# Recurrence levels of 32 tokens and fewer on four 32-column groups of the array, with four masked copies a level

## The chip, the cores and the metric
The program runs on one core of a Trainium2 chip. The metric is the time of one execution on the device in microseconds (us), smaller being better. Before the change three runs gave a median of 1046.14 us (1046.14 to 1046.6). The execution that was profiled took 1045.28 us.

## The reference, cut to what matters
The kernel computes two layers of a hybrid encoder over 512 tokens of width 1024. The part in question is branch C, a gated linear recurrence with 4 heads, key and value width 128, in chunks of 64 tokens:

```python
bcum = jnp.cumsum(gc, axis=2)                     # cumulated log decay in a chunk
diff = bcum[:, :, :, None, :] - bcum[:, :, None, :, :]
decay = jnp.where(causal, jnp.exp(jnp.where(causal, diff, 0.0)), 0.0)
attn = jnp.sum(qc[:, :, :, None, :] * kc[:, :, None, :, :] * decay, axis=-1)
o = einsum('bhts,bhse->bhte', attn, vc) + einsum('bhtd,bhde->bhte', qc * exp(bcum), state)
```

So `attn[t, s]` is a sum over 128 channels of query times key times a decay that depends on both tokens and on the channel.

## The kernel before, in words
Everything is written out by hand for each engine, with semaphores between them. Per layer TensorE runs a list of projection jobs (`JOBS`), most of them 24 matmuls of 128 stationary columns with 512 moving ones (48 with 256 moving ones for `ci` and `bv`, 12 for `mix`), each fp32 product being made of three fp32r matmuls (L480, L481, L482). Results alternate among three PSUM banks `pj`. Between job n and job n+1 TensorE takes the small stages whose turn it is (`hooks[n]`), so these stand in line with the jobs. VectorE (DVE), ScalarE (ACT) and GpSimd (POOL) have lists of phases with the same numbers. `claim` (L474) waits, at the start of a job, for its weights and its bank.

The intra-chunk matrix `attn` is built by levels. For two heads at a time (p = 0, 1) the kernel works on blocks of 128 tokens, two heads by four blocks, so `2 * TB` = 8 blocks, numbered `hb`. Level `lev` has s = 64 >> lev: within each aligned block of 2s tokens it gives the pairs (key in the lower half, query in the upper half). The decay is split at the boundary between the halves: `diffs` (DVE, L1365, L1366), `decay_exp` (ACT, L901) and `operands` (DVE, L1378, L1381) write `XL[lev % 2]`, tile `level_ops`, in which every token's column holds its scaled key or its scaled query. `level` (L587 to L609) on TensorE multiplies them. Level 0 has a form of its own (L599). Levels 1 to 6 (L607) take, for each block `hb` and each half of it, the 64 columns of that half as the stationary operand and the 32 query columns among them as the moving one; the product lands in 64 PSUM partitions and 32 columns of bank `M[3 + lev % 2]`, tile `mx`. Only the entries in which key and query share a block of 2s tokens are wanted.

`take_level` (L1397 to L1420) on DVE copies them into `AT` (tile `attnT`), one `copy_predicated` for each half (L1418): 64 partitions by 8 blocks by 32 columns, with the mask `mask(lev)` of `constants()`, which holds a 1 where the entry is wanted. The other entries stay as they are.

The stages go by job number. With d = 12 for p = 0 and d = 25 for p = 1, the levels follow job d + 1 (diagonal and level 0), d + 3 (levels 1 and 2), d + 5 (levels 3 and 4) and d + 7 (levels 5 and 6), as `PAIRS` says. Their copies stand in DVE's phase with the next number, and behind those of levels 1 to 4, in the same phase, the operands of the next pair, which PE wants two jobs after this one. After the last copies DVE scales keys and queries (`decayed`, L1438, L1440), and TensorE transposes the keys two jobs after the last levels (L616). Before each level `level` waits for `ops_ready` and, for levels 1 to 6, for `at_evac` (L602): that the level two before has been copied out of the bank.

With two layers, two values of p and six levels, L607 is passed 24 times, 16 matmuls each. The operands are plain fp32, and the trace shows such a matmul as two weight loads and two matmuls: 24 x 16 x 2 = 768 of each.

Of the kernel before, what the change touches and what calls it, by code (L numbers as in the profile page):

```python
# [24 lines left out]
P = 128  # L25
KT = D // P
TB = T // P
# [32 lines left out]
GATE_JOBS = [n for n in SG_JOBS if KIND[n] != "bu"]  # L60
BRANCH = {"ag": 0, "bg": 1, "cg": 2}
LEVELS = 7
DIAG = (12, 25)
PAIRS = ((0,), (1, 2), (3, 4), (5, 6))

# [12 lines left out]
def constants():  # L78


    c = np.zeros((P, P + 8 * LEVELS + 8), np.float32)
    masks = c[:, P:P + 8 * LEVELS].view(np.uint8)
    c[:, 0:P] = np.eye(P)
    for lev in range(1, LEVELS):
        s = 64 >> lev
        for i in range(P):
            if i % (2 * s) < s:
                b = i % 64 // (2 * s)
                masks[i, 32 * lev + b * s:32 * lev + (b + 1) * s] = 1
    o = P + 8 * LEVELS  # L90
    freq = np.float32(ROPE_THETA) ** (-np.arange(0, HD, 2, dtype=np.float32) / np.float32(HD))
    c[:, o] = np.tile(freq, P // (HD // 2))
    c[:, o + 1] = np.where(np.arange(P) % HD < HD // 2, -2.0, 2.0)
    return c


def build(nc, x, positions, w_in, b_merge, w_branch, w_out, norm_g, final_g, attn_sinks, sp_w, sp_b,
# [9 lines left out]
    with ctx:  # L107
# [8 lines left out]
        def at(name, shape, offset, dt=f32):  # L116
            return nc.alloc_sbuf_tensor_at(name, shape, dt, offset=offset)
# [44 lines left out]
        AT = at("attnT", [P, 2, T], r_at)  # L162
# [44 lines left out]
        ID = CST[:, 0:P]  # L207
        FREQ, SIGN2 = (CST[:, P + 8 * LEVELS + c:P + 8 * LEVELS + c + 1] for c in (0, 1))

        def mask(lev):  # L210
            return CST[:, P + 8 * lev:P + 8 * (lev + 1)].bitcast(mybir.dt.uint8)
# [11 lines left out]
        def sem(name):  # L223
# [7 lines left out]
            exp_done=4, probs_ready=4, pT_done=4, pT_evac=4, pv_done=4, oa_evac=4, first_zero=1, sig_ready=2,  # L231
            logf_ready=2, c_keys=2, diff_done=2 * LEVELS + 2, decay_ready=2 * LEVELS + 2, ops_ready=2 * LEVELS,
            lev_done=2 * LEVELS + 2, at_evac=2 * LEVELS + 2, khat_ready=2, khT_done=2, khT_evac=2, upd_done=2,
# [150 lines left out]
        def x_bank(k):  # L384

            return (M[2:] + PJ)[k % 6]
# [51 lines left out]
        def _(pe):  # L438

            pe.wait_ge(cst_in, 16)  # L440
            for k in range(KT):
# [5 lines left out]
                for tb in range(TB):  # L447
                    last = pe.transpose(x_bank(k)[:, tb * P:(tb + 1) * P], XTOK[:, tb, k * P:(k + 1) * P], ID)
# [6 lines left out]
            def program(layer):  # L455
# [133 lines left out]
                def level(p, lev):  # L589
                    s = 64 >> lev  # L590
                    pe.wait_ge(ops_ready, upto(ops_ready, LEVELS * p + lev + 1))
                    ops = XL[lev % 2]
                    bank = M[3 + lev % 2]
                    if lev == 0:

                        for hb in range(2 * TB):
                            low, up = (ops[:, hb * P + u * 64:hb * P + u * 64 + 64] for u in range(2))
                            rows = slice(hb % 2 * 64, hb % 2 * 64 + 64)
                            last = pe.matmul(bank[rows, hb // 2 * 64:hb // 2 * 64 + 64], low, up, start=True, stop=True)  # L599
                        last.then_inc(lev_done, 1)  # L600
                        return
                    pe.wait_ge(at_evac, upto(at_evac, (LEVELS + 1) * p + lev))  # L602
                    for hb in range(2 * TB):
                        for half in range(2):
                            blk = ops[:, hb * P + half * 64:hb * P + half * 64 + 64]
                            upper = blk.rearrange("p (b u s) -> p b u s", u=2, s=s)[:, :, 1, :]
                            last = pe.matmul(bank[half * 64:half * 64 + 64, hb * 32:(hb + 1) * 32], blk, upper,  # L607
                                             start=True, stop=True)
                    last.then_inc(lev_done, 1)  # L609

# [79 lines left out]
                for j in range(4):  # L690
                    hooks[ATTN + 3 * j].append((scores, j))
                for p, d in enumerate(DIAG):
                    hooks[d + 1].append((diagonal, p))
                    for i, levels in enumerate(PAIRS):
                        for lev in levels:
                            hooks[d + 1 + 2 * i].append((level, p, lev))
                    for step, f in enumerate((transpose_khat, state_updates, recurrent_out, head_norm)):
                        hooks[d + 2 + LEVELS + step].append((f, p))
# [31 lines left out]
                for n in range(NJ):  # L730
# [7 lines left out]
                    if n == 0:  # L738
# [4 lines left out]
                        for tb in range(TB):  # L743
                            last = pe.matmul(M[3][:, tb:tb + 1], SS[:, tb * P:(tb + 1) * P], ONE[:, 0:1],
                                             start=True, stop=True)
# [9 lines left out]
        def _(act):  # L755
# [50 lines left out]
            def program(layer):  # L806
# [196 lines left out]
                for j in range(4):  # L1003
                    phase[ATTN + 3 + 3 * j].append((probsT_out, j))
                    phase[ATTN + 1 + 3 * j].append((softmax_exp, j))
                for p, d in enumerate(DIAG):
                    phase[FIRST[("cf", p)] + 2].append((forget, p))
# [122 lines left out]
        def _(dve):  # L1130
# [35 lines left out]
            for c, cn, r0 in ((0, 8, 0), (8, 24, 16), (32, 4, 64)):  # L1166
                last = dve.tensor_copy(VL[:, :, c:c + cn],
                                       M[0][:, r0:r0 + 2 * cn].rearrange("p (l c) -> p l c", l=2))
# [60 lines left out]
            def program(layer):  # L1229
# [170 lines left out]
                def take_level(p, lev):  # L1400
                    s = 64 >> lev
                    dve.wait_ge(lev_done, upto(lev_done, (LEVELS + 1) * p + lev + 2))
                    dve.wait_ge(at_evac, upto(at_evac, (LEVELS + 1) * p + lev + 1))
                    src = M[3 + lev % 2]
                    if lev == 0:
                        at5 = AT[:, :, :].rearrange("p h (c v t) -> p (h c) v t", v=2, t=P)
                        for v in range(2):
                            last = dve.tensor_copy(at5[0:64, :, v, 64:128],
                                                   src[v * 64:v * 64 + 64, 0:4 * 64].rearrange("p (c t) -> p c t", t=64))
                        last.then_inc(at_evac, 1)  # L1410
                        return
                    nb = 32 // s
                    at6 = AT[:, :, :].rearrange("p h (c v b u s) -> p (h c) v b u s", v=2, u=2, s=s, b=nb)
                    for half in range(2):
                        rows = slice(half * 64, half * 64 + 64)
                        msk = mask(lev)[rows, :].rearrange("p (b s) -> p b s", s=s).unsqueeze(1)\
                                                .to_broadcast([64, 2 * TB, nb, s])
                        last = dve.copy_predicated(at6[rows, :, half, :, 1, :], msk,  # L1418
                                                   src[rows, 0:2 * TB * 32].rearrange("p (c b s) -> p c b s", b=nb, s=s))
                    last.then_inc(at_evac, 1)  # L1420

                def block_diffs(p):
# [135 lines left out]
                for j in range(4):  # L1558
                    phase[ATTN + 1 + 3 * j].append((neg_max, j))
                for p, d in enumerate(DIAG):  # L1560
                    phase[FIRST[("cf", p)] + 2].append((clamp, p))
                    phase[FIRST[("cf", p)] + 3].append((keys_and_sums, p))
                    phase[d - 1].append((diffs, p, 0))
                    phase[d].append((diffs, p, 1))
                    phase[d].append((operands, p, 0))
                    phase[d + 1].append((operands, p, 1))
                    phase[d + 1].append((diffs, p, 2))
                    phase[d + 2].append((take_diagonal, p))
                    phase[d + 2].append((take_level, p, 0))
                    phase[d + 2].append((operands, p, 2))  # L1570
                    for i in (1, 2):
                        for lev in PAIRS[i + 1]:
                            phase[d + 1 + 2 * i].append((diffs, p, lev))
                        for lev in PAIRS[i]:
                            phase[d + 2 + 2 * i].append((take_level, p, lev))
                        for lev in PAIRS[i + 1]:
                            phase[d + 2 + 2 * i].append((operands, p, lev))
                    phase[d + LEVELS].append((block_diffs, p))
                    for lev in PAIRS[3]:
                        phase[d + LEVELS + 1].append((take_level, p, lev))  # L1580
                    phase[d + LEVELS + 1].append((decayed, p))
                    phase[d + LEVELS + 4].append((states, p))
                    phase[d + LEVELS + 6].append((head_scaled, p))
# [14 lines left out]
                for n in range(NJ + 4):  # L1598
# [9 lines left out]
                    v = layer * NU + JOBS[n][0] + 1 if n < NJ and JOBS[n][1] == 0 else 0  # L1608
# [34 lines left out]
```

## Time and profile before

| | |
|---|---|
| median of three runs | 1046.14 us |
| the profiled execution | 1045.28 us |
| its span, first to last instruction | 1043.4 us |
| TensorE (PE) busy | 1018.4 us, 98% |
| DVE busy | 650.5 us, 62% |
| ACT busy | 521.0 us, 50% |
| mean granted TensorE clock | 0.996 of full |

The span lies inside the execution; 1.9 us of the profiled execution are around it. In the profile PE is TensorE's matmuls, PEld its weight loads, PEldq its sequencer, which passes the instructions on to the array and takes the waits. A row of groups reads: line, engine, operation, tile written <- tiles read, shape, count | busy time, mean of one | idle time before. A matmul's printed duration runs to a modelled end and overlaps its neighbours; what it costs the array is seen from start to start, or in the chain.

### The profile page before, as it was taken

The page shows a single profiled execution, that of the slowest core. Times are in us where ns is not written, and L with a number is a line of the kernel's source. Part 1 is how long each engine was busy: PE and PEld are TensorE (multiplying, and loading weights), DVE is VectorE, ACT ScalarE, POOL GpSimd, SP SyncE. Part 2 cuts the span into 40 slices and gives each one's busy share as a digit, 9 for nine tenths or more (in the row PEclk, how much of TensorE's full clock was granted, in tenths as well). Part 3 has the DMA queues.
Part 4 walks back from the last instruction along what each step waited for, and adds up shares of the span by engine and source line. Part 5 has one row for each costly group of instructions (what it writes and reads, how often), then busy time and mean ns, then how long its engine had stood idle before and what let it go on. Part 6 is the DMA issues. An engine that isn't in the chain of part 4 may idle for free.

```text
span 1043.4 us, 15327 instructions
## 1 busy us (share of the span) xinstructions
PE 1018.4 (98%) x6389; PEld 857.8 (82%) x6389; DVE 650.5 (62%) x832; ACT 521.0 (50%) x809; POOL 302.8 (29%) x156
## 2 busy tenths in 40 slices
PE   5899999999999999999999999999999999999997
PEld 4689899888888888888887889988888888888876
DVE  6876894799635444355548579578984353544552
ACT  5667665676453323232448666577556333332333
POOL 3321111532422313143212110163243232323420
PEclk9899999999999999999999999999999999999999
DMA  6242222222223232333234222122231232323502
GB/s 196 71 129 74 81 83 82 60 62 82 82 61 120 82 101 82 100 101 122 84 114 136 81 83 59 64 82 81 82 101 57 85 102 81 101 81 101 191 12 80
DMA packets 95412, 94.71 MB, mean 91 GB/s; under 512 B 2272, under 2 KB 93616, under 8 KB 95344
## 3 DMA queue, kind: packets, MB, share of 16 engines
q1 hardware_dynamic: 95136, 93.44, 28.9%
q8 instruction: 50, 0.82, 0.3%
q0 software_dynamic: 80, 0.26, 0.2%
q14 instruction: 18, 0.15, 0.1%
q10 hardware_dynamic: 128, 0.04, 0.0%
HBM read 91.64 MB, written 2.10 MB: 90 GB/s over the span
## 4 chain that ended last, share of the span: by engine, by line
PE 95%; DVE 2%; issue 1%; ACT 1%; DMA 1%; POOL 0%; DVEq 0%; POOLq 0%; ACTq 0%
PE pj L480 28%; PE pj L482 27%; PE pj L481 27%; PE mx L607 2%; PE mx L480 1%; PE mx L482 1%; PE mx L481 1%; DVE sum_sq L1196 1%; PE mx L570 1%; PE mx L667 1%; PE mx L547 1%; PE mx L635 1%; PE mx L555 1%; PE mx L645 1%; DMA pos_int<-in_positions 1%
## 5 line engine op out<-in xcount | busy, mean ns | idle before, releaser
L1066 POOL TENSOR_TENSOR w_lo<-w_raw,w_hi 128x512 fp32r<-128x512 f32 (+1 forms) x92 | 198.5, 2158 | 564.5 <-ACT w_hi L783 564.3
L480 PE MATMUL pj<-h_hi,w_hi 128*128 128x512 f32 x832 | 330.7, 397 | 1.5 <-issue 1.5
L482 PE MATMUL pj<-h_hi,w_lo 128*128 128x512 f32 x832 | 325.1, 391 | 0.0
L481 PE MATMUL pj<-h_lo,w_hi 128*128 128x512 f32 x832 | 325.0, 391 | 0.0
L783 ACT ACTIVATE w_hi<-w_raw 128x1024 fp32r<-128x1024 f32 (+1 forms) x184 | 160.6, 922 | 164.3 <-PE pj L482 162.4
L1187 DVE TENSOR_TENSOR w_lo<-w_raw,w_hi 128x512 fp32r<-128x512 f32 (+1 forms) x92 | 159.8, 1737 | 64.9 <-ACT w_hi L783 64.7
L480 PEld LDWEIGHTS pj<-h_hi,w_hi 128*128 128x128 f32 x832 | 156.9, 189 | 36.5 <-issue 4.6
L482 PEld LDWEIGHTS pj<-h_hi,w_lo 128*128 128x128 f32 x832 | 156.7, 188 | 33.3
L481 PEld LDWEIGHTS pj<-h_lo,w_hi 128*128 128x128 f32 x832 | 157.0, 189 | 32.3 <-issue 1.0
L1253 DVE TENSOR_TENSOR merge_gate<-pj,rstd 128x512 f32<-128x512 f32 x48 | 33.2, 691 | 162.9 <-PE pj L482 162.9
L863 ACT ACTIVATE merge_gate<-merge_gate,small 128x512 f32<-128x512 f32 x48 | 34.3, 715 | 89.3 <-DVE merge_gate L1253 89.3
L480 PE MATMUL pj<-branch_hi,w_hi 128*128 128x512 f32 x192 | 75.1, 391 | 0.0
L482 PE MATMUL pj<-branch_hi,w_lo 128*128 128x512 f32 x192 | 74.8, 389 | 0.0
L481 PE MATMUL pj<-branch_lo,w_hi 128*128 128x512 f32 x192 | 74.7, 389 | 0.0
L480 PE MATMUL pj<-w_hi,h_hi 128*128 128x256 f32 x256 | 73.9, 289 | 0.0
L481 PE MATMUL pj<-w_lo,h_hi 128*128 128x256 f32 x256 | 72.4, 283 | 0.0
L482 PE MATMUL pj<-w_hi,h_lo 128*128 128x256 f32 x256 | 72.4, 283 | 0.0
L1066 POOL TENSOR_TENSOR branch_lo<-full,branch_hi 128x512 fp32r<-128x512 f32 x24 | 36.0, 1500 | 94.0 <-ACT branch_hi L950 80.5
L480 PEld LDWEIGHTS pj<-w_hi,h_hi 128*128 128x128 f32 x256 | 49.0, 191 | 0.7
L481 PEld LDWEIGHTS pj<-w_lo,h_hi 128*128 128x128 f32 x256 | 49.0, 192 | 0.0
L482 PEld LDWEIGHTS pj<-w_hi,h_lo 128*128 128x128 f32 x256 | 49.0, 191 | 0.0
L901 ACT ACTIVATE decay<-decay 128x1024 f32<-128x1024 f32 x28 | 29.6, 1067 | 32.9 <-DVE decay L1366 32.2
(240 smaller groups left out, 1526.2 us busy)
## 6 DMA issues: line engine op xcount, KB each, us to landing
w_raw<-in_w_in SPq DMA_DIRECT2D x60, 1024.0 KB, 5.5
w_raw<-in_w_branch SPq DMA_DIRECT2D x24, 512.0 KB, 3.4
w_raw<-in_w_out SPq DMA_DIRECT2D x6, 1024.0 KB, 5.1
x_tokens<-in_x SPq DMA_DIRECT2D x4, 512.0 KB, 9.0
w_raw<-in_w_in SPq DMA_DIRECT2D x4, 512.0 KB, 4.0
w_raw_last<-in_w_out SPq DMA_DIRECT2D x2, 1024.0 KB, 7.3
sp_w_rows<-in_sp_w SPq DMA_DIRECT2D x2, 512.0 KB, 4.7
out<-out_low SPq DMA_DIRECT2D x4, 256.0 KB, 2.0
```

Source lines behind the costliest of these rows:

```text
L480: pe.matmul(bank, wh, ah, start=first, stop=False)
L481: pe.matmul(bank, wh, al, start=False, stop=False)
L482: return pe.matmul(bank, wl, ah, start=False, stop=final)
L547: last = pe.matmul(M[half][rows, cols], QP[d, j, queries], keys[d, held], start=True, stop=True)
L555: last = pe.transpose(M[half][:, tb * P:(tb + 1) * P], PR[:, half, tb, :], ID)
L607: last = pe.matmul(bank[half * 64:half * 64 + 64, hb * 32:(hb + 1) * 32], blk, upper, start=True, stop=True)
L783: act.activation(hi_part(v, half), raw_part(v, half), ACT.Copy).then_inc(w_hi, 1)
L863: act.activation(GM[:, i % 2, t, :], GM[:, i % 2, t, :], ACT.Sigmoid, bias=bm[:, c:c + 1])\
L901: act.activation(E[lev % 2][:, :], E[lev % 2][:, :], ACT.Exp).then_inc(decay_ready, 1)
L1066: return pool.tensor_tensor(out=dst, in0=full, in1=hi.bitcast(f32), op=ALU.subtract)
L1187: dve.tensor_tensor(out=lo_part(v, 1), in0=raw_part(v, 1), in1=hi_part(v, 1).bitcast(f32), op=ALU.subtract).then_inc(w_lo_vec, 1)
L1253: dve.tensor_tensor(out=GM[:, i % 2, t, :], in0=src, in1=RS[:, :], op=ALU.mult)\
```

## The change
Levels 2 to 6 (s of 16 and fewer, so blocks of 32 tokens and fewer) go in quarters of a block of 128 tokens: 32 stationary columns, 16 moving ones, the output in 32 PSUM partitions, so that the four quarters lie on four column groups of the array. DVE takes each of these levels with four `copy_predicated` of 32 partitions. Level 1 stays as it was, level 0 and the diagonal too. In the mask only the number of the column at which a block's entries stand changes.

```diff
+TILE = (P, 64, 32, 32, 32, 32, 32)
@@ constants
-                b = i % 64 // (2 * s)
+                b = i % TILE[lev] // (2 * s)
@@ level, TensorE
+                    w = TILE[lev]
                     for hb in range(2 * TB):
-                        for half in range(2):
-                            blk = ops[:, hb * P + half * 64:hb * P + half * 64 + 64]
+                        for q0 in range(0, P, w):
+                            blk = ops[:, hb * P + q0:hb * P + q0 + w]
                             upper = blk.rearrange("p (b u s) -> p b u s", u=2, s=s)[:, :, 1, :]
-                            last = pe.matmul(bank[half * 64:half * 64 + 64, hb * 32:(hb + 1) * 32], blk, upper,
+                            last = pe.matmul(bank[q0:q0 + w, hb * w // 2:(hb + 1) * w // 2], blk, upper,
                                              start=True, stop=True)
@@ take_level, VectorE
-                    nb = 32 // s
-                    at6 = AT[:, :, :].rearrange("p h (c v b u s) -> p (h c) v b u s", v=2, u=2, s=s, b=nb)
-                    for half in range(2):
-                        rows = slice(half * 64, half * 64 + 64)
-                        msk = mask(lev)[rows, :].rearrange("p (b s) -> p b s", s=s).unsqueeze(1)\
-                                                .to_broadcast([64, 2 * TB, nb, s])
-                        last = dve.copy_predicated(at6[rows, :, half, :, 1, :], msk,
-                                                   src[rows, 0:2 * TB * 32].rearrange("p (c b s) -> p c b s", b=nb, s=s))
+                    w = TILE[lev]
+                    nb = w // 2 // s
+                    at6 = AT[:, :, :].rearrange("p h (c v b u s) -> p (h c) v b u s", v=P // w, u=2, s=s, b=nb)
+                    for v in range(P // w):
+                        rows = slice(v * w, v * w + w)
+                        msk = mask(lev)[rows, 0:w // 2].rearrange("p (b s) -> p b s", s=s).unsqueeze(1)\
+                                                       .to_broadcast([w, 2 * TB, nb, s])
+                        last = dve.copy_predicated(at6[rows, :, v, :, 1, :], msk,
+                                                   src[rows, 0:TB * w].rearrange("p (c b s) -> p c b s", b=nb, s=s))
```

## Rows read from the trace of the kernel before

**Rows 1.** The page: busy times, and the chain that ended last by engine
```profile
PE 1018.4 (98%) x6389; PEld 857.8 (82%) x6389; DVE 650.5 (62%) x832; ACT 521.0 (50%) x809; POOL 302.8 (29%) x156
...
PE 95%; DVE 2%; issue 1%; ACT 1%; DMA 1%; POOL 0%; DVEq 0%; POOLq 0%; ACTq 0%
```

**Rows 2.** Chain of waits around levels 1 and 2: start us, us, what
```profile
129.73 0.88 PE mx L555 x8
130.61 1.99 PE mx L607 x64
132.59 0.31 PE pj L480
```

**Rows 3.** Groups by line and shape, PE and PEld, line L607
```profile
L607 PE MATMUL mx<-level_ops 128*64 128x32 f32 x768 | 24.6, 223 | 0.0
...
L607 PEld LDWEIGHTS mx<-level_ops 128*64 128x64 f32 x768 | 23.4, 138 | 2.7 <-issue 2.4
```

**Rows 4.** Timeline of PE from 130.53, windows ending at 130.58, 130.66, 130.72
```profile
130.54 0.25 PE L607 MATMUL mx<-level_ops 128*64 128x32 f32 x2
...
130.54 0.31 PE L607 MATMUL mx<-level_ops 128*64 128x32 f32 x4
...
130.54 0.37 PE L607 MATMUL mx<-level_ops 128*64 128x32 f32 x6
```

**Rows 5.** Timeline of PE at 76 us: L547, tiles of 64 rows by 64 columns
```profile
76.25 0.32 PE L547 MATMUL mx<-k_rot,q_rot 64*64 64x128 f32 x1
76.26 0.32 PE L547 MATMUL mx<-k_groups_swapped,q_rot 64*64 64x128 f32 x1
76.27 0.27 PE L547 MATMUL mx<-k_rot,q_rot 64*64 64x64 f32 x1
76.27 0.27 PE L547 MATMUL mx<-k_groups_swapped,q_rot 64*64 64x64 f32 x1
...
77.07 0.27 PE L547 MATMUL mx<-k_groups_swapped,q_rot 64*64 64x128 f32 x2
```

**Rows 6.** Stretches, L547 alone, then L607 alone: us, busy (count started), clock
```profile
76.25:76.92 0.67, 0.67 (x34) 0.67 (x38) 1.00 0.00 0
...
115.97:117.00 1.03, 1.02 (x44) 0.91 (x44) 1.00 0.65 119
...
130.53:130.92 0.39, 0.38 (x14) 0.39 (x14) 1.00 0.32 18
```

**Rows 7.** The sequencer's waits (L302 after L547, L602, L577, L302 after L599): duration, start
```profile
L302 PEldq EVENT_SEMAPHORE  x1: 51/51/51, 76.9 to 76.9; - x1
...
L602 PEldq EVENT_SEMAPHORE  x1: 51/51/51, 130.9 to 130.9; - x1
...
L577 PEldq EVENT_SEMAPHORE  x1: 51/51/51, 116.6 to 116.6; - x1
...
L302 PEldq EVENT_SEMAPHORE  x1: 51/51/51, 117.9 to 117.9; - x1
```

**Rows 8.** Chain where levels 5 and 6 follow L570, another 64-column stage
```profile
161.13 1.08 PE mx L570 x32
162.21 1.84 PE mx L607 x64
```

**Rows 9.** DVE by line: the masked copies in two stretches, and plain operations
```profile
L1418 DVE COPY_PREDICATED attnT<-consts,mx x4: 427/438/452, 136.8 to 138.2; 64x256 f32<-64x256 uint8 x4
...
L1418 DVE COPY_PREDICATED attnT<-consts,mx x4: 737/742/747, 163.2 to 165.5; 64x256 f32<-64x256 uint8 x4
...
L1408 DVE COPY attnT<-mx x8: 415/420/425, 121.3 to 723.0; 64x256 f32<-64x256 f32 x8
...
L1394 DVE TENSOR_TENSOR attnT<-mx,consts x8: 683/689/694, 119.8 to 721.8; 64x512 f32<-64x512 f32 x8
```

**Rows 10.** Stretch of p = 1's levels: us, busy us of PE, PEld, DVE, ACT, POOL
```profile
225.00:255.00 30.00, 30.00 (x276) 24.52 (x277) 29.27 (x37) 19.15 (x19) 9.15 (x4) 1.00 0.23 71
```

**Rows 11.** Timeline of DVE: operands of levels 3 and 4, then 5 and 6
```profile
236.29 2.88 DVE L1381 TENSOR_TENSOR level_ops<-query_c,decay 128x512 f32<-128x512 f32 x1
...
250.49 2.89 DVE L1381 TENSOR_TENSOR level_ops<-query_c,decay 128x512 f32<-128x512 f32 x1
```

**Rows 12.** Chain: where PE takes those two pairs of levels
```profile
241.15 1.99 PE mx L607 x64
...
254.24 1.99 PE mx L607 x64
```

**Rows 13.** Timeline after the last levels of p = 1: DVE, then PE
```profile
258.81 3.07 DVE L1418 COPY_PREDICATED attnT<-consts,mx 64x256 f32<-64x256 uint8 x4
261.91 1.20 DVE L1438 TENSOR_TENSOR key_c<-key_c,decay 128x384 f32<-128x384 f32 x2
263.03 1.21 DVE L1440 TENSOR_TENSOR query_c<-query_c,decay 128x1024 f32<-128x1024 f32 x1
...
267.18 0.82 PE L616 MATMUL mx<-consts,key_c 128*128 128x128 f32 x6
```

## Prediction

> **What bounds the kernel now.** The page comes first: PE is busy for 98% of the span and holds 95% of the chain that ended last, DVE is busy for 62% [rows 1]. So a microsecond that TensorE spends in a small stage between two projection jobs is a microsecond of the end, unless an idle time of PE later on takes it up, and all its idle time together is 25 us (1043.4 of the span less 1018.4). Next the chain around a pair of levels: 64 records of L607 in a row, 1.99 us, and then the next job at once [rows 2]. There are 12 such pairs. The groups by line give L607 24.6 us in all for 768 matmul records [rows 3], 32 ns each, and this is all that the change can touch on PE. Its halves already run side by side: by 130.58 two records have started, by 130.66 four, by 130.72 six [rows 4], so two records (one for each column group) start every 0.06 us. The clock is at its full level (2.4 GHz, granted 1.00) in such stretches [rows 6].
>
> **Part 1, TensorE.** Removed: in 20 of the 24 levels, 16 matmuls, which are 32 records of weight load and 32 of matmul. Added: 32 matmuls, 64 and 64 records, each with half the columns on both sides. The question is what a record costs when it is that small and four of them may run at once. No row shows 32 columns, so I bound it.
>
> From below: a round of two column groups takes 0.058 us with 64 columns (64 records, 32 rounds, in about 1.86 us). If a round of four groups with 32 columns took half of that, 0.029 us, a level would be 16 rounds, 0.47 us in place of 0.93. From above: if a record cost what it costs now, 0.029 us, a level would take 64 x 0.029 = 1.86 us.
>
> What decides is how fast the sequencer hands instructions to the array: a level becomes 128 instructions in place of 64. Now 64 instructions in 0.93 us are 14.6 ns each. For 0.47 us they would have to come every 3.6 ns. L547 is the nearest case, since four tiles run at once there: four records of it start within 0.02 us [rows 5]. It has 44 matmuls and 44 loads [rows 6], 88 instructions. At 76.92 us 34 and 38 of them had started [rows 6], 16 were left, and at 76.9 the sequencer was taking the wait that stands behind all 88 [rows 7]. In the levels, where the array is the slower one, the sequencer runs further ahead: at 130.9 it takes the wait of the second level [rows 7] with 28 of the first level's 64 started [rows 6], so with 36 in the queue. I read 36 as the queue's fill when it is full. At 76.25 then at most 36 of the 88 were in it, and the other 52 or more went in during 0.67 us: 12.9 ns each, or 12.2 if it held 33. The second reading: between the waits L577 at 116.6 and L302 at 117.9 [rows 7] lie L585 and L599, 96 instructions, and one wait of 51 ns: (1.3 - 0.05) / 96 = 13.0 ns, with the starts printed to a tenth. There the array could have been what limited, so this is a ceiling of the price. I take 12.5 ns an instruction. That is below the 14.6 ns at which the levels drain now, which is why the limit hasn't shown; it is three times what four groups would ask for.
>
> A pair of levels with 32 columns (3 and 4, 5 and 6; 8 pairs): 256 instructions, 34 of them queued when the first starts, and one wait of 51 ns between the levels. 222 x 12.5 + 51 = 2.83 us from first to last start, against 1.84 (1.99 less the 0.15 of the change of tile shape at its edge; the pair that follows another 64-column stage shows 1.84 [rows 8]). That is +0.99 us, times 8 = +7.9 us.
>
> The pair of levels 1 and 2 (4 of them): level 1 drains as now, 0.93 us, and leaves the queue full. Then the tile shape changes from 64 to 32 columns, for which I take the 0.15 us by which the two pairs of [rows 2, 8] differ. Level 2 then needs (128 - 34) x 12.5 = 1.18 us in place of 0.93. Together +0.4 us each, +1.7 us. And the two pairs that follow L570 [rows 8] now have a change of shape in front of them as well: +0.3 us. Sum on PE: **+9.9 us**.
>
> At 9.4 ns an instruction, the mean over L547 with the head start in it (88 from 76.25 to its last starts near 77.08 [rows 5], 0.83 us), the same sums give +0.3 us for each of the 8 pairs and +0.1 for each of the 4, so +3. At today's 14.6 ns they give +1.45 and +0.6, with the shapes +14.3. Those are the ends for this case.
>
> The Trainium skill, "TensorE: Matmul & The Clock Gate", has in its part on the warmup a floor under small matmuls: start to start never drops below about 25 ns however few columns there are. L547 disagrees as far as it goes (44 records in 0.83 us are 19 ns each, with a full queue at its start); with that floor at every record a level would take 64 x 25 = 1.6 us, and 20 levels would add some 13 us by estimate, which lies inside the ends above.
>
> **Part 2, VectorE.** Removed: 40 copies of 64 x 256. Added: 80 of 32 x 128 elements each. Two plain operations give the parts of a duration: 420 ns for 256 elements, 689 for 512 [rows 9], so 151 ns fixed and 1.05 ns an element. The masked copies take 438 ns at the larger s and 742 at s of 2 and 1 [rows 9]; with half the elements about 295 and 447. Four in place of two: 1.18 for 0.88 us, 1.79 for 1.48, so +0.3 us a level, +6 us of DVE in all, on an engine with 390 us to spare. From the other side, at least nothing, and at most +0.9 us a level if 32 partitions cost as much as 64 x 256. I cost it at nothing for the end, but the cover is thin at p = 1, where DVE is busy for nearly all of the stretch [rows 10]. Two places count. The operands of levels 5 and 6 are ready at 253.38 [rows 11] and PE takes them at about 254.2 [rows 12], 0.8 us later. By then DVE has three more such levels behind it, +0.9 us, while PE has become later by its own pairs 1, 2 and 3, 4, +0.4 and +1.0. So PE comes 1.3 us after them instead of 0.8, and no wait appears; at the dear end (+2.7 us) PE would wait 0.5 us, once a layer. For levels 3 and 4 the gap is 2.0 us (239.17 to 241.15 [rows 11, 12]) against +0.3. Behind the last copies stand L1438 and L1440, which end at 264.24, and the transposes of these keys start at 267.18 [rows 13]: 2.9 us for 0.6 of copies (1.8 at the dear end).
>
> **Part 3, the rest.** The mask has the same size and is built on the host. No DMA, no wait and no order of stages changes.
>
> Sum: the profiled execution's own 1045.28 us + 9.9 = 1055.2. The median of the runs is 0.9 above that execution, so I forecast 1046.14 + 9.9 = **1056.0 us**.
>
> **The rivals.**
> Gain: four groups side by side at the price of their columns. For it: the array overlaps tiles, two in L607 and four in L547 [rows 4, 5], and bursts of records a few ns apart are seen. Against it: the lag of the sequencer behind 88 instructions [rows 6, 7]. It decides if an instruction can be handed over in under 8 ns; there 222 x 8 + 51 ns is today's 1.84. At its best: 16 levels x -0.47 = -7.5, four times -0.47 + 0.15 = -1.3, and +0.3 for shapes: -8.5. But then PE reaches levels 5 and 6 of p = 1 1.2 us earlier (0.3 and 0.9) while DVE is 0.9 later, against 0.8 of cover: PE waits 1.3 us there, in both layers, and gives back 2.6. That leaves -5.9: 1040.2 us. The Trainium skill's same page, in the part on packing small matmuls, speaks for this side: column groups with 32 columns ran at 2.38 times the rate with three tiles. Its case had 512 moving columns, where this one has 16.
> No change: only two of four groups overlap, with half the columns. 32 rounds x 0.029 = 0.93 us, as now, and four changes of shape: +0.9 us, 1047.0. It needs both a quick sequencer and an array that doesn't do four; nothing speaks for that pair.
> Dearer: a round has a fixed price of 0.058 us whatever its columns, and only two groups overlap. A level takes 32 x 0.058 = 1.86 us, +0.93 for each of 20, and the shapes: +19.5, 1065.6. L547, with four tiles at once, speaks against it [rows 5].
>
> **How the numbers follow.** The forecast has 0.75, the gain 0.14, no change 0.05, dearer 0.06. The range starts with the case of no change, takes in the low end of the forecast's price, and ends between the high end (1060.4) and the dearer case: 1046.5 to 1062. It leaves out the gain and nearly all of the dearer case, about 2 in 10. A measurement of this kernel can tell some 0.2% (2.1 us) from no change: faster 0.14, same 0.06, slower 0.80.
>
> **What the profile will show.** If I am right: L607 with 32 columns has 1280 records, and its pairs of levels in the chain stand at about 3.0 us in place of 1.99, the first starts of a pair four abreast and later ones evenly spaced near 25 ns, with the wait behind the pair taken when almost nothing is queued. PE's projection rows stay as they are. L1418 has 88 copies, DVE some 6 us more, and no new wait of PE on DVE at L616. If a pair of levels stands below 1.9 us in the chain, the gain has it and my price of an instruction is wrong.

## Result, and the profile after

The changed kernel takes 1050.72 us (median of 9 runs, 1048.68 to 1053.1), the kernel before 1046.14 (9 runs, 1045.22 to 1046.74): a ratio of 1.0045 [1.0036, 1.0055], +4.6 us. The sign and the range of the prediction held; its size did not, +4.6 us where +9.9 was forecast, and the profile shows that the two figures don't even consist of the same things. The profiled execution took 1050.63 us, with a span of 1048.6. Lines of the kernel have moved on by one to three: L607 is L609 now, L635 is L637, L1381 is L1383, L1418 is L1421, L1453 is L1456.

The page after, against [rows 1]: TensorE is *less* busy, and the chain that ended last runs for 14% over DVE, where it was 2%.

```profile
PE 1015.6 (97%) x7029; PEld 854.1 (81%) x7029; DVE 656.2 (63%) x872; ACT 520.4 (50%) x809; POOL 302.2 (29%) x156
...
PE 77%; DVE 14%; issue 5%; ACT 3%; DMA 1%; POOL 0%; DVEq 0%; POOLq 0%; ACTq 0%
```

The chain of waits after, at the three pairs of levels of p = 0 (start us, us, what; against [rows 2, 8]): the pairs are shorter, 1.72 for 1.99, 1.25 for 1.99, 1.25 for 1.84. The 3.0 us that the prediction wanted here do not exist.

```profile
130.64 1.72 PE mx L609 x84
...
146.34 1.25 PE mx L609 x102
...
161.24 1.25 PE mx L609 x102
```

L609 alone after, in stretches that all begin at 146.30 (us, busy and records started of PE, of PEld, clock): 104 of the 128 matmul records of levels 3 and 4 have started 0.86 us after the first, 8.3 ns each, and as many weight loads beside them. So an instruction starts every 4.1 ns, where the prediction had 12.5.

```profile
146.30:146.60 0.30, 0.30 (x38) 0.30 (x40) 1.00 0.00 0
146.30:147.20 0.90, 0.90 (x104) 0.90 (x106) 1.00 0.00 0
146.30:147.60 1.30, 1.30 (x128) 1.20 (x128) 1.00 0.06 20
```

The sequencer's own waits say the same, without the instructions that were queued before the first start. It takes the wait between levels 3 and 4 (L603) at 146.76 and the one behind level 4 (L303) at 147.36, and 128 instructions lie between them: 0.59 us less the 51 ns of the wait are 4.2 ns each. At 146.76, 118 of the 128 instructions of level 3 have started, so 10 are queued.

```profile
L603 PEldq EVENT_SEMAPHORE  x1: 51/51/51, 146.8 to 146.8; - x1
...
L303 PEldq EVENT_SEMAPHORE  x1: 51/51/51, 147.4 to 147.4; - x1
...
146.30:146.76 0.46, 0.46 (x58) 0.46 (x60) 1.00 0.00 0
```

Where did more than that gain go? Lay the 4320 matmuls of the projections in both traces side by side and note where the distance between their starts changes. Each of the four pairs 1, 2 gains 0.27 to 0.29 us, each pair 3, 4 gains 0.69 to 0.73, each pair 5, 6 of p = 0 0.57 to 0.59, but those of p = 1 at most 0.07. All pairs together: -5.1 us. Three places give it back and more: the recurrent output of p = 1 in layer 0 (+3.98) and in layer 1 (+3.77), and one spot early in a projection job of layer 1 (+2.56). With +0.06 in the start of the kernel the sum is +5.25, the difference of the spans (1048.6 - 1043.4).

PE's waits after (us in total, times, longest) name them, besides the half microsecond per layer for which levels 5 and 6 of p = 1 wait for their operands:

```profile
PE mx L637 <- DVE state L1456: 4.7, 2, 2.4
PE pj L481 <- issue: 3.6, 2, 2.3
PE mx L609 <- DVE level_ops L1383: 0.9, 2, 0.5
```

**The late states.** Timeline after, DVE and PE (start us, us, engine, line, what, idle before it and what ended it). The masked copies of levels 3 to 6 of p = 1 take 2.54 and 3.71 us. L1452 and L1456 make the states that the recurrent output L637 reads; they run behind the weight split L1189, and PE, done with its job at 277.69, stands until 280.06. DVE isn't full just there: ahead of that split it stands for 1.80 us, waiting for ACT's `w_hi`, and the states stand behind the split in its program.

```profile
245.58 2.54 DVE L1421 COPY_PREDICATED attnT<-consts,mx 32x128 f32<-32x128 uint8 x8
...
258.28 3.71 DVE L1421 COPY_PREDICATED attnT<-consts,mx 32x128 f32<-32x128 uint8 x8
...
275.06 2.89 DVE L1189 TENSOR_TENSOR w_lo<-w_raw,w_hi 128x1024 fp32r<-128x1024 f32 x1 [1.80 <-ACT w_hi L785]
...
277.30 0.39 PE L483 MATMUL pj<-h_hi,w_lo 128*128 128x512 f32 x1
...
277.87 0.60 DVE L1452 COPY state<-mx 128x128 f32<-128x128 f32 x2
278.50 1.50 DVE L1456 SCALAR_TENSOR_TENSOR state<-state,decay,mx 128x128 f32<-128x128 f32 x4
...
280.06 0.71 PE L637 MATMUL mx<-attnT,v_c 128*128 128x128 f32 x4 [2.37 <-DVE state L1456]
```

The same place before: the states end 0.24 us later than they do after, and PE comes to them 2.6 us later. It waited for them even so, 0.5 us in each layer, as the loads' waits say (2.8 us in the same rows after, where PE's matmuls show 2.4).

```profile
275.60 2.58 DVE L1187 TENSOR_TENSOR w_lo<-w_raw,w_hi 128x1024 fp32r<-128x1024 f32 x1 [1.41 <-ACT w_hi L783]
...
278.74 1.50 DVE L1453 SCALAR_TENSOR_TENSOR state<-state,decay,mx 128x128 f32<-128x128 f32 x4
...
279.87 0.39 PE L482 MATMUL pj<-h_hi,w_lo 128*128 128x512 f32 x1
280.29 0.71 PE L635 MATMUL mx<-attnT,v_c 128*128 128x128 f32 x4
```

```profile
PEld mx L635 <- DVE state L1453: 0.9, 2, 0.5
```

So of the 2.6 us that PE was ahead at 256 us, it keeps 0.23 at 280. It then loses 1.6 more, with no wait in sight: behind the wait the granted clock is at its half level, 1.2 GHz. Windows of after, then of before (us; busy of PE, PEld, DVE, ACT, POOL; clock); the engine had stood still ahead of 281 us after, and had not before:

```profile
277.70:281.00 3.30, 0.94 (x8) 0.94 (x9) 3.02 (x9) 0.36 (x1) 0.00 (x0) 0.99 0.00 0
281.00:284.00 3.00, 3.00 (x16) 3.00 (x16) 1.00 (x2) 0.27 (x1) 0.00 (x0) 0.50 0.00 0
```

```profile
281.00:284.00 3.00, 3.00 (x28) 2.91 (x27) 1.23 (x2) 0.78 (x2) 0.17 (x1) 1.00 0.03 5
```

**The stop in layer 1.** The timeline after has PE idle for 2.30 us inside a projection job, which waits for nothing:

```profile
668.30 0.28 PE L483 MATMUL pj<-w_hi,h_lo 128*128 128x256 f32 x1
670.87 0.39 PE L481 MATMUL pj<-w_hi,h_hi 128*128 128x256 f32 x1 [2.30 <-issue]
```

The DMA view shows what happened meanwhile. Queue q8 carries instructions, in packets of 16 KB; 55 packets in the whole run, 50 before, and PE is the engine with so many more instructions (1280). From 660 to 668.4 us it moves none, while the 1 MB weight load issued in that stretch runs at up to 390 GB/s; the next packet comes when that load has all but landed (it starts at 668.49 and ends at 669.54), and 1.3 us after its end PE goes on. The stretch 668.4:671 (packets, MB, share of the 16 engines' time):

```profile
q1 hardware_dynamic: 55, 0.04, 5.1%
q8 instruction: 1, 0.02, 2.5%
```

This stop of 2.30 us was not followed by a fall of the clock, where the waits of 2.37 and 2.33 us on the states were:

```profile
671.00:674.00 3.00, 3.00 (x26) 3.00 (x27) 2.45 (x3) 0.00 (x0) 0.00 (x0) 1.00 0.03 5
```

### The profile page after: what moved, and what is told of

Read it like the earlier page. It is cut to its first block, busy times and chain, and to the rows that moved or that the text cites. A ratio compares the mean times of both kernels' runs of the same rounds, so it can differ in the third digit from the quotient of the medians.

```text
span 1048.6 us, 16647 instructions
## 1 busy us (share of the span) xinstructions
PE 1015.6 (97%) x7029; PEld 854.1 (81%) x7029; DVE 656.2 (63%) x872; ACT 520.4 (50%) x809; POOL 302.2 (29%) x156
## 4 chain that ended last, share of the span: by engine, by line
PE 77%; DVE 14%; issue 5%; ACT 3%; DMA 1%; POOL 0%; DVEq 0%; POOLq 0%; ACTq 0%
PE pj L481 23%; PE pj L483 22%; PE pj L482 22%; DVE decay L1368 2%; DVE decay L1367 2%; DVE level_ops L1383 1%; PE mx L481 1%; PE mx L483 1%; PE mx L482 1%; DVE attnT L1421 1%; ACT w_hi L785 1%; DVE level_ops L1380 1%; DVE sum_sq L1198 1%; PE mx L571 1%; PE mx L609 1%
## 5 line engine op out<-in xcount | busy, mean ns | idle before, releaser
L1189 DVE TENSOR_TENSOR w_lo<-w_raw,w_hi 128x512 fp32r<-128x512 f32 (+1 forms) x92 | 160.5, 1745 | 64.8 <-ACT w_hi L785 64.5
```

The costliest lines, as they stand in the source:

```text
L1189: dve.tensor_tensor(out=lo_part(v, 1), in0=raw_part(v, 1), in1=hi_part(v, 1).bitcast(f32), op=ALU.subtract).then_inc(w_lo_vec, 1)
```

## Experiments

The theory after the two traces: quarters on four column groups are a gain of some 7 us on PE, given back by the states of p = 1, which DVE makes late, and the fall of the clock behind that wait, both made worse by the four copies. The rivals: the copies alone make the loss; or PE's loss is in the matmuls themselves. The first runs were the matmuls alone, the copies alone, the states first and the wait filled. The late block of PE's instructions in layer 1 stands in none of their expectations and came into the theory after them, since the run with the states first came out 3 to 4.5 us above what the theory had without it. Each ratio is against the kernel before, measured in turn with the run.

### Matmuls alone

Quarters on PE, placed in the bank so that DVE keeps its two copies of 64 partitions (against the kernel before):

```
-                        for half in range(2):
-                            blk = ops[:, hb * P + half * 64:hb * P + half * 64 + 64]
+                        for q0 in range(0, P, w):
+                            blk = ops[:, hb * P + q0:hb * P + q0 + w]
...
-                            last = pe.matmul(bank[half * 64:half * 64 + 64, hb * 32:(hb + 1) * 32], blk, upper,
+                            c0 = hb * 32 + q0 % 64 // 2
+                            last = pe.matmul(bank[q0:q0 + w, c0:c0 + w // 2], blk, upper,
```

> Levels 2 to 6 as quarters of 32 columns, but each quarter's product is put where the half before had it, so that DVE takes a level with its two copies of 64 partitions as before. Theory (late states): the quarters make TensorE faster (a pair of levels 1.1 to 1.3 us in the chain, not 1.99), DVE's line at p = 1 starts some 1.8 us earlier and isn't lengthened, but TensorE is 3.3 us ahead at the recurrent output, so it waits there about 2 us a layer. 1042.5 us if the clock holds, 1045.7 us if it falls to its half level behind both waits (1.6 us each). Rival (the doubled instructions are what costs): slower than before, 1048 us or more, and no wait on the states. Rival (the extra copies have no part in it): as with the whole change, 1050.7 us.

Measured: 1046.28 us (11 runs, 1044.11 to 1047.07), ratio 0.9999 [0.999, 1.0007]. No loss at all without the copies, and no gain either. The profiled execution, at 1044.25 us, is one of three below 1045; the other eight took 1045.66 to 1047.07, so its trace leaves 2 us of the median unexplained. The theory had 1042.5 us with the clock up and 1045.7 with the clock down behind both waits; in the trace the clock is up, and no trace shows it in the slower executions. The projections laid side by side: 3.1 us ahead at 256 us, then +1.64 at each recurrent output of p = 1 and +1.8 in layer 1, at the stop, which the theory did not have. Its waits:

```profile
PE mx L638 <- DVE state L1456: 3.4, 2, 1.7
...
PE pj L481 <- issue: 3.2, 3, 1.7
```

With DVE's work untouched the states end at 278.79, where it was 280.24 before: 1.45 us earlier, against 3.1 us by which PE is earlier. PE waits for the rest, so half of what it gained is lost there and half is kept. A wait of 1.7 us here left the clock at its full level (281:284 at 1.00).

```profile
277.29 1.50 DVE L1456 SCALAR_TENSOR_TENSOR state<-state,decay,mx 128x128 f32<-128x128 f32 x4
```

### Copies alone

Matmuls as before; levels 2 to 6 taken by four copies of 32 partitions:

```
+                    if lev >= 2:
...
+                        for v in range(4):
+                            rows = slice(v * 32, v * 32 + 32)
...
+                            last = dve.copy_predicated(at6[rows, :, v, :, 1, :], msk, halves_[rows, :, v % 2, :, :])
```

> Matmuls as before, levels 2 to 6 taken by four masked copies of 32 partitions. Theory (late states): DVE's line at p = 1 is 1.7 us longer, TensorE waits for the states 2.2 us in place of 0.5 in each layer, +3.4 us, and +3 more if the clock falls behind the waits: 1049.5 to 1052.5 us. Rival (the doubled instructions are what costs): 1046 to 1047 us, since TensorE's part is as before.

Measured: 1048.18 us (9 runs), ratio 1.0024 [1.0014, 1.0034]. The copies cost +2.2 us at the end, below the theory's range and above the rival's 1047. The trace has two steps, +1.40 and +1.32, both at the states; the wait shows as 1.4 us in the matmuls' rows and 1.8 in the loads', where it was 0.5 before:

```profile
PE mx L635 <- DVE state L1465: 2.8, 2, 1.4
```

The theory had also counted on the clock's fall, and it didn't come (281:284 again at 1.00): after 1.4 and 1.7 us of standing still it stayed, after 2.4 us it fell. One part gives 0.0 us, the other +2.2, both together +4.6: the parts don't add. By the traces they are -1.2, +2.7 and +5.25, 3.75 more together than in sum; some 3.0 of it is the clock, which falls only behind the wait that both lengthen, and 0.75 the stop in layer 1, which is longer with both.

### States first

The whole change, and DVE makes the states ahead of the weight split of that phase:

```
+                    ahead = [x for x in phase[n] if x[0] is states]
+                    for f, *a in ahead:
+                        f(*a)
...
-                        f(*a)
+                        if f is not states:
+                            f(*a)
```

> The whole change, and DVE takes the states of p = 1 ahead of the split of the next weights instead of behind it. Theory (late states): the states are ready near 275.4 instead of 280.0, TensorE comes at 277.6 and does not wait, the clock holds, and the 3.3 us that the matmuls give in each layer reach the end: 1039.5 to 1041 us. Rival (the doubled instructions, or the copies as such): 1049 to 1051 us, nothing gained. Rival (the wait only moves): TensorE waits later for the weights that now come after the states, at most 2 us a layer: 1043 to 1045 us.

Measured: 1044.02 us (9 runs), ratio 0.9976 [0.9966, 0.9985]: 6.7 us below the change as it was, and now faster than before by 0.2%, but above the 1039.5 to 1041 us of the theory. (Three of the nine took 1041.83 to 1042.25; no trace shows how they differ.) The states now end at 275.65, since DVE makes them in the time in which it waited for ACT's `w_hi`, and no wait of PE on them is left. What is left is the stop in layer 1, now 2.6 us long, and here the clock falls behind it:

```profile
PE pj L481 <- issue: 4.1, 3, 2.6
...
PE mx L609 <- DVE level_ops L1383: 0.9, 2, 0.5
```

```profile
665.00:667.00 2.00, 0.00 (x0) 0.00 (x0) 1.97 (x4) 0.00 (x0) 0.62 (x1) 1.00 0.03 4
667.00:670.00 3.00, 2.89 (x14) 2.89 (x15) 2.46 (x3) 0.00 (x0) 0.00 (x0) 0.57 0.02 5
```

Stop and slow stretch together cost 4.3 us there, which is what the theory lacked. The record behind it has the same number in PE's program as the one behind the stop of after, though PE gets there 4 us earlier: the stop hangs on a place in the instruction stream, not on a time.

### The kernel before with the states first

The same edit on the kernel before, the control for it.

> The kernel before with the states of p = 1 ahead of the split of the next weights. Theory: its TensorE waited 0.5 us for the states in each layer, and only that can go: 1045.0 us. Rival (the order itself gives the gain that the run with the whole change and the states first showed): 1042 us or less.

Measured: 1045.18 us (11 runs), ratio 0.9993 [0.9984, 1.0002]: not told from no change by the interval, though the trace has the two steps that go with the 0.5 us waits, -0.3 us each. The rival, by which the order itself would have given 1042 us or less, is out. So the order of DVE was worth little until the change leaned on it.

### The wait filled

The whole change; PE does 10 matmuls for nobody where it would stand and wait for the states (they run from 278.82 to 281.1):

```
+                    if p == 1:
...
+                        for i in range(FILL):
+                            pe.matmul(M[2][:, 0:P], ID, ID, start=True, stop=True)
```

> The whole change, and TensorE does 10 idle matmuls (128x128 by 128, into a bank that nobody reads, about 2.2 us) ahead of its wait for the states of p = 1. Theory (late states, then the clock): the wait was idle time, so the fill costs nothing, and the clock stays at its full level behind it: 1.5 us less a layer, 1047.5 us. Rival (the clock has no part in it): 1050.7 us, as with the change.

Measured: 1051.84 us (5 runs), ratio 1.0056 [1.0042, 1.007]. This kernel is for the clock. The states are as late as ever, but the steps there are +2.39 and +2.33 in place of +3.98 and +3.77: 1.6 and 1.4 us less, and the clock stays up (first row). The total went up all the same, against the 1047.5 us of the theory. With 40 more instructions ahead of it the same record number now falls inside a pair of levels, PE stands for 3.6 us, and the clock is down for longer (third row); that spot costs 6.2 us in place of 2.56.

```profile
276.00:290.00 14.00, 13.84 (x86) 12.22 (x85) 6.65 (x10) 4.49 (x9) 4.65 (x3) 1.00 0.05 16
666.00:670.00 4.00, 0.66 (x4) 0.62 (x4) 1.40 (x4) 1.71 (x2) 2.34 (x1) 0.79 0.56 193
670.00:676.00 6.00, 6.00 (x33) 6.00 (x33) 5.35 (x9) 0.00 (x0) 0.00 (x0) 0.57 0.01 3
```

```profile
PE mx L610 <- issue: 3.6, 1, 3.6
```

### Weight loads held

The whole change; SP waits for the pair of levels before it issues the three weight loads of a layer that would start with a pair of p = 0:

```
-                    sp.wait_ge(pj_done, jobs_to(max(w for w in range(v) if slot(w) == slot(v))))
+                    after_job = jobs_to(max(w for w in range(v) if slot(w) == slot(v)))
+                    sp.wait_ge(pj_done, after_job)
+                    in_layer, lay = (after_job - 1) % NJ, (after_job - 1) // NJ
+                    if in_layer in (DIAG[0] + 3, DIAG[0] + 5, DIAG[0] + 7):
+                        sp.wait_ge(lev_done, counted(lay)(lev_done, in_layer - DIAG[0] + 1))
```

> The whole change as it is, and only the three loads at p = 0 held. Theory: the stall of layer 1 goes (2.5 us), the late states stay with 2.4 us of wait and a fallen clock in each layer: 1048.2 us. Rival (the stall only hid part of the wait for the states): 1050.7 us.

Measured: 1047.48 us (11 runs), ratio 1.0012 [1.0003, 1.002]. Against the trace of after the whole difference in the middle of the run is one step of -2.56 us at the place of the stop, which is gone. The edit touches neither PE's instructions nor DVE, only when a load goes out. (The medians differ by 3.2 us; the profiled execution, 1048.41 us, is the slowest of the eleven.) The packet of instructions (below, the stretch 665.8:666.9) now goes out ahead of the load, from 665.81 to 666.80 us, and PE comes to the place at 668.5. In the four traces that have the stop (matmuls alone, the change, states first, the wait filled) PE goes on 1.3 to 1.5 us after the packet's end; here that time is over before PE arrives.

```profile
q8 instruction: 1, 0.02, 5.6%
```

The wait on the states is what it was:

```profile
PE mx L641 <- DVE state L1460: 4.7, 2, 2.4
```

### States first and loads held

Both edits on the whole change.

> The whole change with the states first (1044.02 us), and at p = 0 the three weight loads that start together with a pair of levels wait until that pair is done (about 1.2 us each). Theory (late instructions): in the run before, TensorE stood still for 2.6 us behind levels 5 and 6 of layer 1, always at the same instruction, until a block of its own instructions arrived, which went out only when the weight load begun at the pair's job had landed; then the clock fell for 3.4 us. With the load held the block comes in time: no stall, no fall, 4.3 us less, 1039.7 us. Rival (the stall is a matter of the instruction rate, not of the load): the stall stays, 1044 us. Rival (the weights come late in turn): TensorE waits for w_lo, 1044 us or more.

Measured: 1040.75 us (5 runs), ratio 0.9944 [0.9931, 0.9958], 3.3 us below the states first alone. The stop and the slow stretch are gone. Of PE's new waits one is left:

```profile
PE mx L613 <- DVE level_ops L1387: 0.9, 2, 0.5
```

### All three

Quarters placed for two copies of 64 partitions, states first, loads held: the fastest version.

> Quarters of 32 columns, but DVE's old two copies a level, the states first and the loads held. Theory (matmuls gain, DVE's line and the instruction blocks take it back): nothing is in the way, the eight pairs give 0.73 us each and the four others 0.27, 7 us in all: 1039 us, and up to 1 us below the run with the four copies, in which TensorE waits for the operands of levels 5 and 6 (0.9 us in two waits). Rival (the copies cost at the end too): 2 us or more below the run with the four copies.

Measured: 1038.36 us (5 runs, 1038.13 to 1039.41), ratio 0.9928 [0.9915, 0.994], 7.5 us below the kernel before and 12.4 below the change. No wait of PE on states, operands or instructions is left, and the pairs 3, 4 and 5, 6 of p = 1, which the chain showed at 1.99 us each [rows 12], stand in its chain with 1.26 and 1.25 us:

```profile
239.53 1.26 PE mx L614 x101
...
251.89 1.25 PE mx L614 x101
```

Its trace is 6.96 us shorter than that of before: 6.5 from the twelve pairs, 0.6 from the states. The kernel with four copies is 2.4 us slower. Laid side by side, 1.45 us of it is levels 5, 6 of p = 1, whose operands come late with four copies (0.69 and 0.76 in the two layers); the other 1.0 lies in the first 65 us, where the clock came up later in that profile, before any level runs. So the rival's 2 us or more is met by the medians, and 1.45 us of it is the copies' by the traces.

## Why the prediction was right or wrong

**The price of an instruction: wrong, and with it the reason for the loss.** The prediction read 12.5 ns from the wait that stands behind L547 and from the stretch L577 to L302 [rows 5, 6, 7], and took the sequencer for what limits. Measured is 4.1 ns from start to start (104 matmuls and 106 loads in 0.86 us) and 4.2 ns by the prediction's own method, between the sequencer's waits. That is below the 8 ns that the prediction itself named as the point of decision, and levels 3 and 4 take 1.25 us where it had 2.83. Its sum of +9.9 us on PE was -6.5 us by the version that lets it show. The step that failed is the inference from queue depth: it took 36 for the fill at the first start of L547, and the 16 records left at the wait for the sign of a sequencer that can't keep up. The second reading, which it rightly called a ceiling since the array could have been the limit there, was then used to support the value. Why the wait behind L547 is taken with 16 records left stays open; a slow sequencer isn't the reason, since after, at 4.2 ns each, the wait between levels 3 and 4 is taken with 10 left. The 0.15 us for a change of tile shape was right: the pairs 5, 6 of p = 0, behind L570, gain 0.58 us where the others gain 0.73.

That the time still came out slower, and inside the range, is luck: the loss was forecast on PE, which gained, and it arose at places that the forecast had at nothing.

The Trainium skill, "TensorE: Matmul & The Clock Gate", part 1, has start to start never below about 25 ns. Across four column groups the rows show a matmul record every 8.3 ns; the rule, if it holds for one tile after another, doesn't hold for tiles side by side. The figure for packing that the Trainium skill has on the same page, which the prediction weighed on the other side, has its sign borne out: four groups with 16 columns each beat two with 32.

**The rival of the gain: the right mechanism, and too few of its consequences.** It had 16 levels at -0.47 and the mixed pairs and shapes besides, -8.5 at best; measured -6.5 for all pairs. A pair doesn't halve from 1.84 to 0.9: 38 matmul records start in the first 0.26 us (6.8 ns each), the next 66 in 0.6 us (9.1 ns), which fits a sequencer that becomes the limit once the queued instructions are used up; that wasn't tried by itself. The rival also foresaw the wait for the operands of levels 5 and 6 of p = 1, priced at 1.3 us; it took 0.5 us of idle time and all of that pair's gain of 0.7.

**DVE: the sizes right, "I cost it at nothing for the end" wrong.** 88 copies, +5.7 us of DVE for +6 forecast; by line and shape after:

```profile
L1421 DVE COPY_PREDICATED attnT<-consts,mx 32x128 f32<-32x128 uint8 x80 | 28.4, 355 | 9.1 <-PE mx L609 7.0
...
L1421 DVE COPY_PREDICATED attnT<-consts,mx 64x256 f32<-64x256 uint8 x8 | 3.5, 442 | 0.1
```

The cover was checked at two places (the operands, and the transposes, where indeed no wait came), and the third wasn't: the recurrent output L635 of p = 1, 20 us on, behind the states. Its row was in the trace, a wait of 0.5 us in each layer, and that means cover below nothing: whatever DVE gets later there, the end gets. By the run with the copies alone this was worth +2.2 us. And past that place a *faster* PE keeps only as much as the states themselves come earlier: by the run with the matmuls alone 1.45 us of 3.1.

**The clock: not thought of.** A wait grown from 0.5 to 2.8 us (2.4 in the matmuls' rows) brought a stretch at half clock behind it, 1.6 and 1.4 us in the two layers; the filled wait shows it, as the difference of the steps.

**PE's instruction blocks: not thought of.** The prediction said that no DMA changes. PE's own instructions are 640 more of each kind, which is five more packets of q8 (55 for 50), and one of these blocks falls behind a weight load at a time when PE goes through 256 instructions in 1.1 us. That the load's timing decides is shown by holding it (2.56 us gone, nothing else moved); that what PE lacks is the block is read from the fixed place in the stream and from the packet, whose end comes 1.3 to 1.5 us before PE goes on in all four traces with the stop; it wasn't tried by itself. The Trainium skill, "Runtime: NRT & Kernel Launch", has under "Instruction fetch mechanics" that the cost of crossing such a block is mostly hidden; here, beside a dense pair and behind a 1 MB load, PE stood for 1.7 to 3.6 us.

**Balance of the change** in its profiled execution, us: twelve pairs -6.5 were to be had, 1.4 of it lost on the operands of p = 1 (two pairs at 0.7), late states and the clock +7.75 (some 3.0 of it the clock; with no wait on the states it would be -0.6), the instruction block +2.56: -5.1 + 7.75 + 2.56 = +5.2.

## What to carry to other kernels

Before you make a small stage of the bounding engine faster, list every wait that it already has on a helper behind that stage, tiny ones too. A wait of half a microsecond says that the helper sets the time there, that a faster engine keeps past it only what the helper gets earlier too, and that work added to the helper ahead of it is paid. Look also at what the helper itself waits for just ahead of the work in question. Then reorder the helper first; here that and holding three loads turned +4.6 us into -5.1, and leaving the helper's copies as they were into -7.5. Read an instruction's price from a stage whose instructions are the dense ones, or call it unknown; queue positions at one wait don't give it.

## What the runs showed of the hardware that was not expected

Tiles of 32 columns start four abreast on four column groups, and a matmul record with its load takes 8.3 ns in a full stretch, against 29 before [rows 3, 4]; the sequencer hands over an instruction every 4.2 ns. Stops of PE of 1.4, 1.7 and 2.30 us left the clock at 2.4 GHz, stops of 2.33, 2.37, 2.6 and 3.6 us were followed by stretches at 1.2 GHz, so between 2.30 and 2.33 us the length alone doesn't tell the two apart. PE stood still for 1.7 to 3.6 us, with nothing to wait for in the program, where a packet of instructions came behind a large load; where in the run that happens moves with the number of instructions ahead of it, so that ten idle matmuls early in the program made a stop later on longer by 1.3 us.
